# Layer 1 of a two-layer mixer and mixture-of-experts trunk: expert rows picked by TensorE, results summed in PSUM

## The reference

```python
def grouped_moe(h, router_w, router_b, w_gate, w_up, w_down):
    ...
    gates = jnp.sum(jax.nn.one_hot(expert_idx, N_EXPERTS, dtype=jnp.float32) * w[..., None], axis=1).astype(h.dtype)
    out = jnp.zeros_like(h)
    for e in range(N_EXPERTS):
        a = jax.nn.silu(h @ w_gate[e]) * (h @ w_up[e])
        out = out + gates[:, e:e + 1] * (a @ w_down[e])
    return out
...
        y = grouped_moe(h2x.reshape(-1, d), router_w, router_b, w_gate, w_up, w_down)
        x = x + g2 * y.reshape(b_, n, d)
...
    return rms_norm(x, final_g)
```

## Time and profile before

| | us |
|---|---|
| median of 3 runs | 1079.36 |
| lowest, highest | 1078.83, 1083.41 |
| the profiled execution | 1075.46 |
| its span in the trace | 1073.7 |
| layer 1's first gate/up product begins | 806.66 |
| first looped weight load of layer 1 issued | 810.66 |
| last down product of layer 1 ends | 1042.5 |
| last DVE instruction ends | 1065.88 |

### The profile page before, as it was taken

The page is one execution under the profiler, slowest core; times in us unless marked ns, Lnnn a source line. Parts: engine busy times, 40 slices in busy tenths (PEclk is TensorE's granted clock), DMA queues, the critical chain, the costliest instruction groups (busy, mean ns, idle before and its releaser), DMA issues.

```text
span 1073.7 us, 20956 instructions
## 1 busy us (share of the span) xinstructions
PE 837.7 (78%) x8079; PEld 495.8 (46%) x8079; DVE 350.0 (33%) x777; ACT 170.0 (16%) x398; POOL 181.4 (17%) x335
## 2 busy tenths in 40 slices
PE   3799999898994899979876729999946655566760
PEld 2237433666443477745544517867423322223430
DVE  2204110866245333323221245367253211012213
ACT  3210100434011111101100133034011000001001
POOL 2000200001401233323222130000010211012202
PEclk9899999999996999989988959999968886679995
DMA  9987778729958699999999945646269999999923
GB/s 346 379 290 274 275 274 331 291 84 389 390 191 296 240 392 394 393 400 395 393 389 404 375 161 183 232 173 245 78 245 391 403 412 415 414 412 401 404 107 118
DMA packets 92516, 332.32 MB, mean 310 GB/s; under 512 B 14576, under 2 KB 36480, under 8 KB 67872
## 3 DMA queue, kind: packets, MB, share of 16 engines
q1 hardware_dynamic: 65920, 289.80, 69.5%
q0 software_dynamic: 14624, 33.38, 8.6%
q10 hardware_dynamic: 11904, 8.14, 2.5%
HBM read 302.11 MB, written 29.26 MB: 309 GB/s over the span
## 4 chain that ended last, share of the span: by engine, by line
PE 46%; DMA 39%; DVE 7%; issue 3%; ACT 1%; SPq 1%; POOL 0%; ACTq 0%; DVEq 0%; POOLq 0%
DMA weight_ring<-in_w_up_dram 18%; DMA weight_ring<-in_w_gate_dram 16%; PE bank L1034 8%; PE bank L1037 8%; PE bank L1150 8%; PE bank L1227 6%; DMA weight_ring<-in_w_mod_dram 4%; PE bank L956 3%; PE bank L1239 3%; PE bank L1112 3%; PE bank L1085 3%; PE bank L1097 2%; PE bank L1256 1%; DMA weight_ring<-y_by_expert,slot_numbers 1%; DVE qk_tokens L1636 1%
## 5 line engine op out<-in xcount | busy, mean ns | idle before, releaser
L1227 PE MATMUL bank<-weight_ring,qk_tokens 128*32 128x256 f32 x3968 | 260.0, 413 | 71.1 <-DMA weight_ring<-in_w_up_dram 62.8
L1227 PEld LDWEIGHTS bank<-weight_ring,qk_tokens 128*32 128x32 f32 x3968 | 153.1, 118 | 169.6 <-issue 103.2
L1239 PE MATMUL bank<-weight_ring,qk_tokens 128*32 128x256 f32 x1984 | 136.4, 415 | 50.5 <-DVE qk_tokens L1653 50.4
L717 POOL DMA_DIRECT2D qk_tokens<-h_by_expert x216 | 107.5, 498 | 345.9 <-DVE qk_tokens L1642 277.5
L1642 DVE STREAM_TRANSPOSE qk_tokens<-qk_tokens 128x256 f32<-128x256 f32 x54 | 35.0, 649 | 299.1 <-PE bank L1227 299.1
L1239 PEld LDWEIGHTS bank<-weight_ring,qk_tokens 128*32 128x32 f32 x1984 | 74.6, 118 | 102.8 <-DVE qk_tokens L1653 63.4
L1034 PE MATMUL bank<-weight_ring 128*128 128x256 f32 (+1 forms) x320 | 97.1, 462 | 4.9 <-ACT weight_ring L802 3.1
L1037 PE MATMUL bank<-weight_ring 128*128 128x512 f32 (+1 forms) x256 | 84.9, 489 | 0.0
L1150 PE MATMUL bank<-weight_ring 128*128 128x512 f32 x192 | 83.4, 594 | 1.4 <-ACT weight_ring L871 1.4
L908 ACT ACTIVATE qk_tokens<-bank 64x256 f32<-64x256 f32 x62 | 23.3, 376 | 374.4 <-PE bank L1227 374.4
L1034 PEld LDWEIGHTS bank<-weight_ring 128*128 128x128 f32 x320 | 61.5, 195 | 40.0 <-issue 34.6
(11 more groups left out here) (171 smaller groups left out, 627.8 us busy)
## 6 DMA issues: line engine op xcount, KB each, us to landing
weight_ring<-in_w_gate_dram SPq DMA_DIRECT2D x64, 1024.0 KB, 8.5
weight_ring<-in_w_up_dram SPq DMA_DIRECT2D x64, 1024.0 KB, 8.5
weight_ring<-in_w_down_dram SPq DMA_DIRECT2D x64, 1024.0 KB, 8.4
weight_ring<-in_w_mod_dram SPq DMA_DIRECT2D x24, 2048.0 KB, 8.3
weight_ring<-in_w_in_dram SPq DMA_DIRECT2D x12, 1024.0 KB, 10.1
h_by_expert<-qk_tokens POOLq DMA_DIRECT2D x17, 512.0 KB, 10.8
weight_ring<-in_w_out_dram SPq DMA_DIRECT2D x4, 2048.0 KB, 11.5
y_by_expert<-qk_tokens ACTq DMA_DIRECT2D x248, 32.0 KB, 5.7
```

The costliest lines, as they stand in the source:

```text
L717: pool.dma_start(hrow[i][q * SLOTS:(q + 1) * SLOTS, :], hsort[bass.ds((n * 2 + (AHEAD + i)) * SLOTS, SLOTS), q * Q:(q + 1) * Q]).then_inc( ...
L1227: mm = pe.matmul(pb[0][32 * g:32 * g + 32, 0:Q].rearrange("p (c f) -> p c f", c=2), hTe[:, k * SLOTS:(k + 1) * SLOTS], w[:, k, :].rearrang ...
L1239: mm = pe.matmul(pb[4][32 * g:32 * g + 32, 0:Q], aTe[:, k * SLOTS:(k + 1) * SLOTS], wdown(n)[:, k, g * Q:(g + 1) * Q], start=(k == 0), sto ...
```

## The change

Layer 0 does the same work as before. In layer 1 neither `hsort` nor `ysort` is used, and all tiles go through one loop, in which each engine does per tile:

- TensorE: gate/up product (now bank 1); then `add_to_sums` for the tile *before*: 8 matmuls that multiply `spread` (which token takes which of the tile's rows, with the gate's weight) by the scaled results, on four row groups of the array (32 rows, 128 columns each), adding into banks 2 to 5; then `pick` for the *next* tile: 8 matmuls of a one-hot matrix with `h2` into bank 6; then the down product (bank 0).
- DVE: product, turn, turn of the next rows from bank 6, the next one-hot (3 instructions), `spread` from rows of token places and weights (4 instructions), and, when the down product is done, its scaling by `g2` into `ysb`.
- ACT: SiLU only. POOL: nothing.

Banks 2 to 5 begin with the residual: four matmuls with the identity (`start_sums`), two of them before the prefix matmuls, two behind. The places and weights of the tokens get on all partitions by two matmuls of ones with diagonals (`token_rows`) before the first gate/up product. At the end ACT and DVE read the finished sum straight from the banks. `final_g` and `g2` are loaded ahead of expert 2's `up` part. Several semaphores are merged.

The diff, cut to its core:

```diff
@@ SP
+                else:
+                    for j in range(AHEAD):
+                        sp.dma_start(g2q[j * SLOTS:(j + 1) * SLOTS, :],
+                                     mod_d[l, 0, 5 * D + j * Q:5 * D + (j + 1) * Q].partition_broadcast(SLOTS)).then_inc(s_g2q, 16)
+                    sp.dma_start(vbuf[:, :], final_g.partition_broadcast(P)).then_inc(s_fg, 16)
...
@@ POOL
+                if l + 1 == DEPTH:
+                    nc.gpsimd.memset(ones, 1.0)
+                    nc.gpsimd.memset(spread, 0.0).then_inc(s_sp, 1)
+                    nc.gpsimd.memset(ysb[0], 0.0).then_inc(s_y[l], 1)
+                    continue
...
@@ ACT
+                if l + 1 == DEPTH:
+                    for i, row in enumerate((place_rows, gate_rows)):
+                        act.wait_ge(s_bc, i + 1)
+                        nc.scalar.copy(row, pb[7][:, :].rearrange("p (k t) -> p k t", k=2)).then_inc(s_bcA, 1)
...
+                    with act.Fori(0, total) as T:
+                        silu(T)
+                    continue
...
-                act.wait_ge(s_comb.sem, s_comb.at(l, t + 1))
-                nc.scalar.activation(hr(l, t), xres[:, t, :], ACT.Square, accum_out=st[:, 0, t:t + 1]).then_inc(s_ssf, 1)
+                act.wait_ge(s_sum, total + 1)
+                nc.scalar.activation(quarters_of(hr(l, t)), final_x(t), ACT.Square, accum_out=st[:, 0, t:t + 1]).then_inc(s_ssf, 1)
...
@@ PE
+                def pick(T):
+
+                    pe.wait_ge(s_oh, T + 1)
+                    for t in range(NX):
+                        for j in range(AHEAD):
+                            mm = pe.matmul(pb[6][32 * j:32 * j + 32, 0:Q], onehot[:, t, :], h2[:, t, j * Q:(j + 1) * Q],
+                                           start=(t == 0), stop=(t == NX - 1), tile_position=(0, 32 * j))
+                    mm.then_inc(s_pk, 1)
+
+                def add_to_sums(T, last):
+
+                    pe.wait_ge(s_sp, T + 2)
+                    pe.wait_ge(s_y[l], T + 2)
+                    for t in range(NX):
+                        for j in range(AHEAD):
+                            mm = pe.matmul(pb[2 + j][:, t * Q:(t + 1) * Q], spread[32 * j:32 * j + 32, t * P:(t + 1) * P], ysb[0][32 * j:32 * j + 32, :],
+                                           start=False, stop=last and t == NX - 1, tile_position=(32 * j, 0))
+                    mm.then_inc(s_sum, 1)
...
+                if l + 1 == DEPTH:
+                    start_sums(2)
+                    start_sums(3)
+                    pe.wait_ge(s_route.sem, s_route.at(l, 2))
+                    hi = first_tile_index(1)
+                    pick(0)
+                    pe.wait_ge(s_sp, 1)
+                    token_rows(0, place_diag)
+                    token_rows(1, gate_diag)
+                    lo = 0
+                    for e in range(NE):
+                        with pe.Fori(lo, hi) as T:
+                            gate_up(T, l + e, e // RING + 1, True)
+                            add_to_sums(T - 1, False)
+                            pick(T + 1)
+                            down(T, l + e, e // RING + 1, True)
+                        lo = hi
+                        if e + 2 <= NE:
+                            hi = first_tile_index(e + 2)
+                    add_to_sums(hi - 1, True)
+                    continue
...
@@ DVE
+                    with dve.Fori(0, total) as T:
+                        product(T)
+                        turn_a()
+                        turn_picked(T + 1)
+                        next_one_hot(T * 4 + 2)
+                        for k in range(2):
+                            ins = V.scalar_tensor_tensor(out=hits[:, k], in0=place_rows[:, k], scalar=place, in1=gate_rows[:, k],
+                                                         op0=ALU.is_equal, op1=ALU.mult)
+                        chain(ins, T * 4 + 5)
+                        dve.wait_ge(s_sum, T + 1)
+                        V.tensor_tensor(spread, hits[:, 0], hits[:, 1], ALU.add).then_inc(s_sp, 1)
+                        chain(V.tensor_scalar(place, place, float(SLOTS), None, ALU.add), T * 4 + 6)
+                        dve.wait_ge(s_d[l], T + 1)
+                        V.tensor_tensor(ysb[0], down_bank(l)[:, 0:Q], g2q, ALU.mult).then_inc(s_y[l], 1)
+                    continue
```

More of the change, by code:

```diff
@@ L381, in hybrid_trunk @@
         s_first = Stage(sem('s_first_rows_picked'), 1)
-        s_hrow = [lsem(f's_hrow_{i}') for i in range(2)]
+        s_hrow = [sem(f's_hrow_{i}') for i in range(2)]
         s_hT = lsem('s_hT')
@@ L913, in store_rows @@
                     if stored is not None:
[L914 to L915 removed]
+                        act.wait_ge(s_yd[i], stored * 64)
+                    nc.scalar.copy(ysb[i], down_bank(l)[:, 0:Q]).then_inc(s_y[l], 1)
                     act.wait_ge(s_y[l], T + 2)
@@ new lines, in token_rows @@
+                def token_rows(i, diag):
+                    pe.wait_ge(s_diag, i + 1)
+                    if i > 0:
+                        pe.wait_ge(s_bcA, i)
+                    pe.matmul(pb[7][:, :], ones, diag, start=True, stop=True).then_inc(s_bc, 1)
+                if l + 1 == DEPTH:
+                    start_sums(2)
[18 more added lines that the diff above has]
+                    continue
```

246 lines of the change are left out of this document (148 added, 98 removed).

## The result

The changed kernel took 1037.46 us (median of 4 runs, 1031.9 to 1039.12) against 1079.09 for the kernel before on the same chip: ratio 0.959, 95% interval 0.9567 to 0.9614. The direction was right and the size too small: 41.6 us of gain by the medians, where 34.9 were forecast.

The account below looks back on a forecast made before the run. Layer 1 was taken as bound in turn by the start chain, weight transfers, the tile chain and the tail: 3.3 + 8.5 + 6.6 + 16.5 = 34.9 us off 1075.46, plus 3.9 to the median, gives 1044.5; range 1037 to 1056.

Parts of the forecast that it names:

- (a): Layer 1 from routing to the first tile: shorter DVE chain and pick start gate/up sooner, 3.3 us saved (1.5 to 5.2).
- it comes behind about 2 us of work with holes: First gate/up product: after so little TensorE work it runs partly at 1.2 GHz, taking 3.7 to 7.4 us.
- (b): Layer 1 stretch bound by weight transfers: row traffic goes and frees the DMA engines, 8.5 us saved.
- Rival 3: Weight stretch: memory, not the DMA engines, is the limit; the 8.5 us comes back partly or wholly, 1049 to 1053; 8%.
- (c): Tiles 12 to 21: sums and pick fill TensorE's wait and hold its clock, 7.44 us per tile, 6.6 us saved.
- that costs nothing: Wait between gate/up and down product: sums and pick, taken as 1.0 us, fit into its 2.05 us.
- rival 2: Tile chain: small matmuls run one after another, or DVE's chain is longer than its parts; 12.6 us lost, 1057; 10%.
- rival 1: Tile chain: the clock keeps falling because the wait is only half filled; the 6.6 us is missing, 1051; 20%.
- Rival 4: Tile chain: TensorE's clock stays at 1.2 GHz throughout, 15.5 us per tile, 80.6 us more, 1125; 3%.
- (d): Tail after the last down product: 14.7 us instead of 31.2, 16.5 us saved (15 to 17).
- the end gap: Tail, from the last DVE instruction to the end of the span: taken as unchanged at 7.8 us.

Follow-up runs that it names:

- after_trimmed: Changed kernel with the second token_rows matmul in a free bank, not awaiting ACT's copy, and DVE scaling before the next one-hot: 1033.13 us, ratio 0.9591 to the kernel before.
- the runs with the two halves: Changed kernel with only ACT's four unused 32 KB stores per layer 1 tile put back, 1043.13 us, or only POOL's four unused loads, 1052.94 us.
- after_rows_travel: Changed kernel with POOL's four loads and ACT's four stores per tile of layer 1 put back, their data unused: 1058.14 us.
- before_filled: Kernel before, with 16 unused column-tile matmuls of constants between each layer 1 tile's gate/up and down product: 1075.97 us against 1080.34, ratio 0.9963.
- after_pick_twice: Changed kernel with the 8 matmuls of each pick issued twice, with the same result: 1044.76 us.
- after_late_gather: Changed kernel with two unused gathers of 128 rows on POOL's queue put back near tile 17 of layer 1: 1038.03 us.

## Why the prediction came out as it did

**(a) The start: right in kind, 1.3 too little.** The first gate/up was to come about 5.2 us sooner and to run at the low level for part of its 3.7 to 7.4 us. It came 4.6 us sooner and took 3.64, at clock 1.00. The 0.6 us that it came later than forecast are a wait that the prediction had wrong: the second `token_rows` matmul waits not for its diagonal (ready at 803.78) but for ACT's copy out of bank 7 (done at 804.44), and after_trimmed, without that wait, begins its first product 0.9 us sooner. The step that failed on the clock is "it comes behind about 2 us of work with holes". Behind it, yes; but the clock had already risen at 798, and stayed up over the holes. Before it rose, TensorE had been busy 3.88 of 5 and 4.00 of 4 us, some 3 of the last 4 with the matmuls that begin the sums. Of the changed kernel, in order of time, these (L1254), two of them at either level:

```profile
793.20 3.76 PE L1254 MATMUL bank2to<-residual,consts_sb 128*128 128x512 f32 x4
...
797.89 1.96 PE L1254 MATMUL bank2to<-residual,consts_sb 128*128 128x512 f32 x4
```

The kernel before, the same place up to the end of its pick, columns as in the earlier trace rows:

```profile
793.00:798.70 5.70, 1.46 (x6) 1.36 (x6) 4.39 (x21) 0.00 (x0) 0.63 (x1) 0.50 0.04 16
798.80:804.80 6.00, 5.96 (x8) 2.31 (x8) 1.31 (x9) 0.00 (x0) 3.26 (x4) 0.61 0.83 272
```

There TensorE was idle most of the wait and the clock rose only in the 6.01 us pick. The prediction put the four matmuls at no cost, and in time they have none (the slot numbers are final 46.7 us behind the start of the output projection before, 46.6 after); that they leave a high clock for the pick and the first tile it had not seen. Whether it was they that raised it, no run with them elsewhere showed. Their price was mis-sized as well, like the pick's below: I had 0.86 us each at the low level, and it is 1.9 there and 1.0 at the high one.

**(b) The weight stretch: right.** 7.9 for 8.5, and the chain still holds weight transfers only. Rival 3, no gain here, fell. That the row traffic lengthens the stretch is shown from the other side too: 12.9 us come back when the rows travel again. It isn't the bytes alone: 1.50 MB of stores took 4.7 us of the engines, where as much of weights takes 3.6. The working had split the gain evenly by share; in the runs with the two halves a load on POOL's queue costs nearly twice its share and a store on ACT's little more than its own. Why putting the rows back costs 12.9 where taking them away gave 8.6 (up to tile 12) is not settled. The number of loads isn't it: 44 fall into the stretch before and 45 in after_rows_travel. Most of the difference is in the weight packets, 2.49 us per MB there and 2.45 before; so loads on POOL's queue don't always slow the weights as much as in these runs, and why is open.

**(c) The tile chain: right by luck in its core.** Forecast 7.44 per tile, measured 7.26. The mis-sized term is the pick, and the sums' lower bound with it. I took 32 rows of the profile for a down product, 1.93 us, and counted the pick as 8 of them, 0.48. But the 8 are of the written program, and the profile counts each twice, as the note behind the order of TensorE's instructions says. (The 64 and 32 matmuls of the two products, as the part on the kernel before names them, are records of the profile too.) The pick is 16 records and takes 1.00 us. The sums take 1.08, between my bounds of 0.48 and 1.73. Together 2.08 for the 1.0 that I took.
The wait was mis-read as well. The terms 3.50, 2.05 and 1.93 add up to 7.48 and not 7.44; in the rows the wait is 2.11 in one tile (973.65 to 975.76) and 2.01 in the tile of 7.44. And it did not stay: with DVE's turn moved behind, it is 1.8 us, so that 2.08 go into 1.8, "that costs nothing" does not hold by 0.3, and only the products that no longer start behind a gap (3.45 for 3.50, 1.73 for 1.93) bring the tile below 7.44. That sums and pick came to about the old wait is luck. Had I counted passes on both sides, rival 2 (serial small matmuls) would have been 3.46 + 1.0, 2.4 above the wait in every tile, and would have deserved more of a chance and a longer range.
Since TensorE never stops, the clock question of rival 1 did not come up, the 0.2 us that a down product takes longer behind a gap is gone as well (1.93 to 1.73), and tile 11 gains too; these make 9.0 of 6.6. before_filled shows the clock part by itself: 8.1 to 7.5 per tile at clock 1.00, with the order unchanged and the weights late. Rival 4, a clock that stays at 1.2 GHz, fell: 1.00 over 72.9 us.
The two changes of tiling mode per tile, which the Trainium skill ("TensorEngine Tiling (Array Packing)", Key Properties) says drain the engine, may cost more than the 0.1 us that I had estimated from the skill's figures: 16 records of column tiles take 0.86 us in a stream without such a change (the second pick of after_pick_twice), the pick behind the sums 1.00 and the sums 1.08. So the two changes and the row tiles' own price are 0.36 us together at most; no run here separates them.

**(d) The tail: the end gap was not in it.** The forecast was 14.7 us, of which 7.8 "as before" from the last DVE instruction to the end of the span. That step failed: it was 3.3. It is the largest part of the miss: 4.5 us less gain would have put the result inside the range, which let the tail's saving vary only from 15 to 17. Up to the last DVE instruction the tail came as forecast, 7.2 us behind the last down product for "some 7". This time came back with POOL's loads, and with nothing else that was tried. The runs fit 0.081 us for each load of layer 1 on POOL's queue, of which the first 28 or so are hidden: 4.55, 6.34 and 8.13 for 44, 66 and 88. Before, there were 72 loads, for which the fit gives 6.8, and 8 indirect transfers; it took 7.8. The last 1.0 may be the indirect ones, which was not tried beyond the two gathers of after_late_gather (3.3). The rest is small and partly cancels: the last scale ends 1.2 us behind the down product instead of 0.5, because DVE, behind the one-hot, is still at the hits and `spread` of a tile that does not exist (rows 1023.88 to 1025.12); the sums take 1.3 with their hand-over instead of 1.1; the two squares 2.2 instead of 2.6, since the second begins beside the read-out of the first; the outputs 2.5 instead of 2.7.

**The scale of the medians.** The forecast added 3.9 us, the distance of the first profiled execution from its median. That holds for the kernel before. The profiled execution of the changed one was close to its own median (1037.04 and 1037.46), so the difference of medians, 41.6, is near the 42.2 of layer 1 and not the 38.6 of the two spans.

## What to carry to other kernels

- Fill a wait on the engine that is the bound with work that the next tile needs anyway, and measure the wait in the new order: here 2.08 us went into a wait that had been 2.05 and was now 1.8, and the same work on the other side of the product cost 2.8 us per tile. A second copy of one part, added as a test, tells at once whether there is room left.
- When a duration is taken from the profile's records and a count from the program, bring both to the same unit before multiplying.
- Where the DMA engines are saturated, small transfers cost more than their bytes, and filling a wait without taking the traffic away gained only 4.4 us where 6 to 8 were expected; look at the time behind the last instruction as a term of its own, since it changed with the traffic of the whole layer.

## What the runs showed of the hardware

- The end of the span comes behind the landing of the output by a time that the program sets. With up to 22 loads on POOL's queue in layer 1 it came 3.3 us behind the last DVE instruction, with 44, 66 and 88 it came 4.55, 6.34 and 8.13 behind it; 88 stores on ACT's queue left it at 3.35. Behind the landing nothing shows on any engine. Whether transfers of layer 0 count too, was not tried.
- Beside four unused loads of 32 KB per tile on POOL's queue a MB of weights took 2.51 us of the DMA engines instead of 2.43 to 2.44; beside stores of the same size on ACT's queue 2.44. The kernel before, with both, had 2.45.
- In the chain of waits a gate/up and a down product took 3.45 and 1.73 us in a gapless stream of TensorE, behind a gap 3.71 and 1.93. The timeline has the gate/up product at 3.64 in both cases; in the stream it starts 0.18 us before the records of the product ahead end (980.81 and 980.99).
